# The output bias of windowed attention, added inside the projection's matmul groups instead of after them

## The reference, cut to what matters

```python
# layers 0 and 3, inside swa_attention
return out.reshape(bsz, seq, SWA_HEADS * SWA_HEAD_DIM) @ w_o + b_o      # [256,1024] @ [1024,1024] + [1024]
# layers 1 and 2 end in the same product without a bias: return o @ w_o
# in the block, for every mixer result m:
h = h + rmsnorm(m, g[3])            # y = m * rsqrt(mean(m*m) + eps) * g
ff = swiglu(rmsnorm(h, g[4]), ffn_w_in[layer, 1], ffn_w_out[layer, 1])
```

## Time and profile before

| what | value |
|---|---|
| median of three runs | 3320.06 us |
| the profiled execution: its time | 3318.66 us |
| the profiled execution: its span, first to last instruction | 3316.8 us |
| mean granted TensorE clock | 0.934 |
| TensorE matmul busy | 2943.9 us (89%) |
| VectorE busy | 1969.6 us (59%) |
| ScalarE busy | 1427.1 us (43%) |
| DMA, mean over the span | 142 GB/s |

### The profile page before, as it was taken

How to read it: one execution, slowest core, us unless ns; L and a number is a source line. 1 busy time by engine, 2 the same in 40 slices (tenths; PEclk the granted TensorE clock), 3 DMA queues, 4 the chain that set the end, 5 groups by cost and what they waited for, 6 DMA issues and landing times.

```text
span 3316.8 us, 43927 instructions
## 1 busy us (share of the span) xinstructions
PE 2943.9 (89%) x17510; PEld 2574.8 (78%) x17510; DVE 1969.6 (59%) x2350; ACT 1427.1 (43%) x1782; POOL 33.4 (1%) x19
## 2 busy tenths in 40 slices
PE   8987999998499999666887799998799999999998
PEld 6876787878388788665876688887688787988887
DVE  5665666663756665556455566666566665655565
ACT  4454445443344544442221344545444544444444
POOL 0000000000000000000000000000000000000000
PEclk9998999998699999786998799999899999999999
DMA  8643555644056565330000465664365564752663
GB/s 241 199 127 99 175 177 176 196 131 154 0 178 190 165 192 179 112 91 1 1 1 21 122 189 170 188 183 127 102 196 169 174 194 126 210 162 94 188 189 95
DMA packets 625086, 471.49 MB, mean 142 GB/s; under 512 B 41441, under 2 KB 592737, under 8 KB 624948
## 3 DMA queue, kind: packets, MB, share of 16 engines
q1 hardware_dynamic: 620292, 460.01, 46.1%
q10 hardware_dynamic: 4656, 9.56, 0.9%
HBM read 466.63 MB, written 1.84 MB: 141 GB/s over the span
## 4 chain that ended last, share of the span: by engine, by line
PE 77%; DVE 13%; ACT 4%; issue 2%; PEldq 1%; DMA 1%; DVEq 1%; ACTq 0%; SPq 0%; PEld 0%
PE pair_bank L371 25%; PE pair_bank L372 13%; PE pair_bank L519 11%; PE out_banks L384 6%; PE out_banks L386 6%; PE out_banks L385 6%; PE out_banks L519 3%; DVE low L306 1%; DVE mix L1947 1%; PE pair_bank L1788 1%; ACT high L302 1%; PEldq L228 1%; PE pair_bank L1801 1%; DVE h L654 1%; DVEq L228 1%
## 5 line engine op out<-in xcount | busy, mean ns | idle before, releaser
L306 DVE TENSOR_TENSOR low<-raw,high 128x3072 fp32r<-128x3072 f32 (+3 forms) x328 | 935.2, 2851 | 787.1 <-ACT high L302 785.2
L371 PE MATMUL pair_bank<-x_parts,high 128*128 128x512 f32 x3520 | 1240.5, 394 | 10.9 <-DVE x_parts L702 8.4
L372 PE MATMUL pair_bank<-x_parts,low 128*128 128x256 f32 x3520 | 987.4, 281 | 0.0
L302 ACT ACTIVATE high<-raw 128x3072 fp32r<-128x3072 f32 (+3 forms) x328 | 774.5, 2361 | 341.7 <-PE out_banks L386 193.4
L371 PEld LDWEIGHTS pair_bank<-x_parts,high 128*128 128x128 f32 x3520 | 662.0, 188 | 166.9 <-issue 14.1
L372 PEld LDWEIGHTS pair_bank<-x_parts,low 128*128 128x128 f32 x3520 | 668.2, 190 | 9.2
L411 ACT ACTIVATE sq_scratch<-pair_bank 128x512 f32<-128x512 f32 x220 | 131.7, 599 | 585.1 <-PE pair_bank L372 585.1
L384 PE MATMUL out_banks<-high,hid_h 128*128 128x512 f32 x880 | 348.5, 396 | 4.0 <-DVE hid_l L447 4.0
L385 PE MATMUL out_banks<-low,hid_h 128*128 128x512 f32 x880 | 348.0, 395 | 0.0
L386 PE MATMUL out_banks<-high,hid_l 128*128 128x512 f32 x880 | 347.9, 395 | 0.0
L519 PE MATMUL pair_bank<-x_parts,high 128*128 128x256 f32 x1216 | 234.2, 295 | 40.5 <-DVEq L228 32.0
(11 more groups left out here) (350 smaller groups left out, 3121.8 us busy)
## 6 DMA issues: line engine op xcount, KB each, us to landing
raw<-in_ffn_w_in_dram SPq DMA_DIRECT2D x352, 512.0 KB
raw<-in_ffn_w_out_dram SPq DMA_DIRECT2D x176, 512.0 KB
raw<-in_ffn_w_dram SPq DMA_DIRECT2D x132, 512.0 KB
raw<-in_w_in_dram SPq DMA_DIRECT2D x32, 1024.0 KB
raw<-in_gla_w_in_dram SPq DMA_DIRECT2D x12, 1024.0 KB
raw<-in_rwkv_w_rkv_dram SPq DMA_DIRECT2D x12, 1024.0 KB
raw<-in_swa_w_qkv_dram SPq DMA_DIRECT2D x10, 1024.0 KB
raw<-in_swa_w_o_dram SPq DMA_DIRECT2D x8, 1024.0 KB
```

Of the source, the lines that this page charges most:

```text
L302: nc.scalar.activation(high[u % SPLIT][:, lo:w], raw[u % RAW][:, lo:w], ACT.Copy).then_inc(high_ready, count)
L306: nc.vector.tensor_tensor(low[u % SPLIT][:, lo:w], raw[u % RAW][:, lo:w], high[u % SPLIT][:, lo:w].bitcast(F32), ALU.subtract).then_inc(we ...
L371: nc.tensor.matmul(o, H[:, w], x_parts[:, k, :], start=(k == 0), stop=False)
L372: last = nc.tensor.matmul(o[:, 0:SEQ], L[:, w], xh[:, k, :], start=False, stop=(k == KB - 1))
```

## The change

In layers 0 and 3 each of the 8 result groups of the output projection is opened by one more matmul: the contraction has a single row, the stationary operand is `ones[0:1, 0:128]`, the moving operand the 256 bias values of the chunk on partition 0. Both are float32, not fp32r. The first regular matmul of the group then accumulates instead of starting. The crossing's `post` part gets `bias=None`, so that it takes the form without a bias in both functions. The bias is loaded to one partition (4 KB) and no longer broadcast to 128 (512 KB), at the same place of the same queue.

```diff
@@ class Stage: a new field bias_row=None @@
@@ proj_pe @@
-                        last = nc.tensor.matmul(o, a, b, start=(j == 0), stop=(j == len(terms) - 1))
+                        if j == 0 and st.bias_row is not None:
+                            nc.tensor.matmul(o, ones[0:1, 0:P], st.bias_row(mix, slice(0, 1))[:, c * CH:c * CH + n],
+                                             start=True, stop=False)
+                        last = nc.tensor.matmul(o, a, b, start=(j == 0 and st.bias_row is None), stop=(j == len(terms) - 1))
@@ swa @@
-             (bo, spread(io["swa_b_o"][j])),
+             (lambda mix: bo(mix, slice(0, 1)), io["swa_b_o"][j:j + 1, :]),
...
-              Stage("proj", chunks=columns(io["swa_w_o"][j], 0, D), feature_major=False, dest="out", evac=None, x=attended_x),
-              Stage("post", gain=post_gain, norm=True, scale=1.0, bias=bo)]
+              Stage("proj", chunks=columns(io["swa_w_o"][j], 0, D), feature_major=False, dest="out", evac=None, x=attended_x,
+                    bias_row=bo),
+              Stage("post", gain=post_gain, norm=True, scale=1.0, bias=None)]
```

More of the change, by code:

```diff
@@ L36, in __init__ @@
                  items=0, max_blocks=0, setup=None, post=None, pre=None, turn=False, pe=None, act=None, dve=None,
-                 columns=None, beside_pe=None, beside_act=None, beside_dve=None, beside_sp=None, x=None, x_wait=None):
+                 columns=None, beside_pe=None, beside_act=None, beside_dve=None, beside_sp=None, x=None, x_wait=None, bias_row=None):
         self.kind, self.loads, self.setup = kind, list(loads), setup
@@ L48, in __init__ @@
         self.beside_pe, self.beside_act, self.beside_dve, self.beside_sp = beside_pe, beside_act, beside_dve, beside_sp
-        self.x, self.x_wait = x, x_wait
+        self.x, self.x_wait, self.bias_row = x, x_wait, bias_row
         self.units = FB + 1 if kind == "ffn" else len(chunks)
```

## The result

| | before | changed |
|---|---|---|
| median of seven runs | 3319.82 us (3314.44 to 3322.04) | 3333.74 us (3327.68 to 3336.56) |
| ratio changed / before | | 1.004, 95% interval 1.0028 to 1.0051 |
| the profiled execution: its time, its span | 3318.66, 3316.8 us | 3334.5, 3332.6 us |
| mean granted TensorE clock | 0.934 | 0.932 |

The change makes the kernel slower, as forecast, but by 13.9 us between the medians (9 to 17 us by the interval), where the forecast was +9.4 and the range ended at 3332.5 us. The time is 1.2 us outside. The means of the same seven runs are 13.2 us apart, 3332.15 us for the changed kernel.

A forecast was written before the change was run, and what follows sets the result against it. TensorE was taken to bound the projections, VectorE and ScalarE the crossings. Sixteen products add 12.9 us, the crossings give back 3.5: +9.4, so 3328.1 us profiled, 3329.5 median; range 3325.5 to 3332.5 us.

The forecast's parts named there:

- What bounds the stage: Output projections of layers 0 and 3: TensorE runs without a gap, so work added to its stream adds to the path.
- The crossing: Behind each projection, dropping the bias additions cuts TensorE's idle time from 8.35 to 6.60 us, 1.75 a layer.
- The product: One bias product in the projection costs 0.83 us: 0.43 stream plus about 0.40 for changing the number of rows.
- The first product of a layer: Behind a wait at the projection's start, it costs 0.65 us in both layers, 1.2 as upper end.
- The load: Bias load at 129 us: 512 KB less frees DMA time that nobody waits for; zero effect.
- The step that failed: Sum over both layers' projections and crossings, 12.9 us more less 3.5, taken as +9.4 us for the whole kernel.
- The third rival: The clock costs more: one more projection stretch at the low level adds 2.3 us, +11.7 in all, 3331.8 us; 12%.
- two-stretch end: Upper case of the clock-costs-more rival: two such low-clock stretches, 3334 us.
- the crossing's shorter wait would help the clock: Argument against the clock costing more: the shorter wait in the crossing helps by 0.24 us a layer.

The follow-up runs named there:

- full-rows kernel: The change, but each bias product multiplies the identity by the bias broadcast to 128 rows; 1.0012 of the kernel before, mean +3.7 us.
- the change twice: The changed kernel in its seven runs and timed again with no edit; 1.0040 and 1.0043 of the kernel before, means +13.2 and +15.6 us.
- layer 3 only: The whole change made in layer 3 alone, layer 0 as before; 1.0031 of the kernel before, mean +10.2 us.
- layer 0 only: The whole change made in layer 0 alone, layer 3 as before; 1.0032 of the kernel before, mean +10.9 us.
- both tiles in front: The changed kernel with the bias products of a chunk's two tiles back to back at the chunk's start; 1.0050 of the kernel before, mean +16.2 us.
- the two in which GpSimd was at work: The change with GpSimd splitting the bias for fp32r products, opening each group or run in the wait before the projection; 1.0020 and 1.0011 of before.
- crossing-only kernel: The kernel before with the new crossing and no bias products, the output bias left out; 0.9983 of before, mean -5.0 us.
- products-only kernel: The change's 16 one-row products, but the crossings keep their old form and still add a tile; 1.0039 of the kernel before, mean +12.5 us.
- the pair in the gap: The change with four 512-column fp32r products of a GpSimd-split bias in TensorE's wait before each projection; 1.0011 of the kernel before, mean +2.3 us.

## Why the prediction was wrong

*What bounds the stage*: right. TensorE has no gap in the projection, and every microsecond put on it shows.

*The crossing*, -1.75 a layer: right, 6.60 us of idle time in all kernels that have the new form, and -5.0 (interval -2.7 to -8.6) for the two alone.

*The product*, 0.83: measured 0.81. The sum of 0.43 for the stream and 0.40 for going in and out holds in each part: 0.43 alone in the full-rows kernel, 1.25 for two with one change to one row and back. *The first product of a layer*, 0.65: 6.46 - 7 x 0.81 = 0.79 in layer 0, and (31.06 - 24.75) - 7 x 0.81 = 0.64 in layer 3 when profiled again. The steps as a whole: +9.4 as forecast.

*The load*, nothing: from 128 to 136 us TensorE is again busy 8.00 of 8.00, with the DMA engines at 0.77 instead of 0.92.

*The step that failed* is the sum, "12.9 us more in the projections, 3.5 less in the crossings: +9.4 us", carried over to the whole kernel as it stands: it ended at the edges of the two stages, and put the change of the other 3200 us at nothing without a reason. It wasn't nothing. In the profiled pair 5 us stand there (and 1.3 more in layer 3's projection, which was 31.06 us when profiled again), and in the means of the runs 4 to 6. The third rival named it and priced its two-stretch end at 3334 us, where the median is; its chance of 12% was too small, and its end was left out of the range. That the number fits is in part luck: no two stretches of 2.3 us stand in the profile, but several of 0.7 to 1.9, and not all of them came again. That the crossing's shorter wait would help the clock, its argument against, holds for the crossing alone (-5.0) and not with the products.

What is shown of the cause is a pattern and not yet a mechanism. The kernels that have a one-row product as the first matmul of a projection together with the new crossing (the change twice, layer 3 only, layer 0 only, both tiles in front) are 4 to 10 us over their steps. All with 128-row products in front, or regular matmuls, are within 2 us of them, but for the two in which GpSimd was at work. Moving the products off the front, and pairing them, took the excess away; with eight changes of rows in either kernel, the place alone makes 1.3 to 1.4 us in each projection. In the pieces that could be laid side by side it is TensorE at 1.2 GHz for longer, with the same instructions.

What stays open: why the kernel with the products and the old crossing has no excess, though its layer-0 projection took 32.45 us at 0.90 (its GLA mixer, 3.7 us shorter than the change's, makes up for it in the profile, and is not explained either); how far the place of the products counts with 16 changes of rows, as the change has them; why the clock then falls otherwise in GLA's mixer, 400 us behind the change, and how much that explains (the crossing-only kernel has a mixer of 203.7 us too, and no excess); and why a change in layer 3 alone costs 5.5 us over its steps. In its profile 0.7 us of that stand ahead of anything that it changes, in layer 0's first FFN, 2.0 in the hybrid mixer, which differs by 4 to 5 us between executions of one kernel, and 1.9 behind the last FFN, where the span ends 6.3 us after the last store is issued instead of 4.4. The change touches no instruction in any of these places. The Trainium skill ("TensorE: Matmul & The Clock Gate", "What's actually happening") puts the moment of the clock's rise down to the phase of the clock gate when the kernel starts and calls the penalty less than 1% of a span. The size agrees, 1% being 33 us; but the same kernel twice gave the same lengths within 0.2 us in the projection of layer 0 and in GLA's mixer, so the phase alone does not explain these.

## What to carry to other kernels

A small product in a dense TensorE stream is priced by its columns and, as much again here, by the change of its number of rows (0.43 and 0.38 us), not by its work: put such products side by side, between two groups, or give them all 128 rows, and try them away from the first place behind a wait. Work out the touched stages from rows, and then keep for the untouched ones a term of some tenths of a percent in the range, on the side on which TensorE has more to do at the low clock. A helper on GpSimd is not free because GpSimd is idle: look at which VectorE operations stand beside it.

## What the runs showed of the hardware

- An fp32 product of 256 columns costs TensorE 0.43 us on 128 rows and 0.81 on one row in a stream of 128-row fp32r matmuls; two on one row together 1.25.
- With two one-row products (four instructions) at the start of layer 0's projection the granted clock is full 7.7 us behind that start, in both profiles; with a regular matmul, a 128-row product or a single one-row product it is 4.2 to 4.6 us, but 6.5 in the products-only kernel. In layer 3 it was 7.4 us with two products, and with the change's single one 6.2 in the first profile and 4.1 in the second.
- With four fp32r products of 512 columns in the 1.85 us of waiting ahead of a projection (the pair in the gap), the clock is full from the projection's second matmul in both layers.
- GLA's mixer, with the same instructions in all kernels, took one of three lengths in 14 profiles, 199.7, 201.6 or 203.5 us (each within 0.2), and the same one again in both kernels that were profiled twice.
- VectorE's 128x4 operation of 0.16 us took 1.90 to 1.92 beside a two-input GpSimd operation of 2.33 us, and ended with it, in four places.
